# Taking a vector-matrix product off TensorE during a chunked scan: ACT scales the weight blocks, POOL adds them

## The reference, cut to what matters

```python
def second_block(x, c, w_mod, b_mod, g_mix_norm, ...):
    mod = jax.nn.silu(c) @ w_mod[l] + b_mod[l]        # (1, 1024) @ (1024, 6144)
    sh_m, sc_m, gt_m, sh_f, sc_f, gt_f = [m[:, None, :] for m in jnp.split(mod, N_MOD, axis=-1)]
    h = rms_norm(x, g_mix_norm[l]) * (1.0 + sc_m) + sh_m
```

## Time and profile before

| | us |
|---|---|
| runs | 1657.38, 1660.76, 1661.72 |
| profiled execution, its own time | 1656.79 |
| its span, first to last instruction | 1655.0 |
| PE busy over the span | 1355.6 |
| DVE busy | 1017.8 |
| ACT busy | 404.4 |
| POOL busy | 289.1 |
| scan of four chunks, from the first product to the last state | 204.1 to 354.5 |
| behind the scan, to the next block | 354.5 to 376.7 |

### The profile page before, as it was taken

One profiled execution on the slowest core, in us unless ns is written; L12 is line 12 of the kernel. 1 busy time (PEld: TensorE's weight loads), 2 busy tenths in 40 slices (PEclk: granted clock), 3 DMA queues, 4 the chain that ended last, 5 costly groups with the idle time before them and its releaser, 6 DMA issues. The chain is left out here.

```text
span 1655.0 us, 18102 instructions
## 1 busy us (share of the span) xinstructions
PE 1355.6 (82%) x6762; PEld 928.1 (56%) x6762; DVE 1017.8 (62%) x2352; ACT 404.4 (24%) x842; POOL 289.1 (17%) x297
## 2 busy tenths in 40 slices
PE   4796789997888787877877878765799968799988
PEld 2783477767853332332322223223688857699988
DVE  0597377774867868786868696542422487455542
ACT  1513300014521010101010101003523434554431
POOL 0002100000124343434443434420000000000000
PEclk9897798899899999999999999996899989899989
DMA  9346831137179999999999999992244205434543
GB/s 400 151 152 251 327 124 61 51 130 291 53 276 419 415 422 412 422 417 421 401 423 407 422 410 421 421 423 125 89 166 160 95 1 204 153 129 177 203 153 128
DMA packets 48184, 426.59 MB, mean 258 GB/s; under 512 B 5344, under 2 KB 5472, under 8 KB 5600
## 3 DMA queue, kind: packets, MB, share of 16 engines
q0 software_dynamic: 36864, 268.45, 39.4%
q1 hardware_dynamic: 11232, 156.98, 24.4%
HBM read 424.36 MB, written 1.05 MB: 257 GB/s over the span
## 5 line engine op out<-in xcount | busy, mean ns | idle before, releaser
L1232 PE MATMUL bank<-arena 128*128 128x512 f32 x1024 | 512.7, 638 | 151.6 <-DVE arena L1328 151.5
L1232 PEld LDWEIGHTS bank<-arena 128*128 128x128 f32 x1024 | 189.2, 199 | 470.2 <-DVE arena L1328 299.7
L1352 DVE CUSTOM_DVE_ANT_0 arena<-arena 128x1024 f32<-128x1024 f32 x256 | 313.1, 1223 | 176.0 <-DMA arena<-experts_in,arena 175.5
L1185 POOL DMA_INDIRECT arena<-experts_in,arena x256 | 268.3, 1048 | 629.1 <-PE bank L1232 373.5
L459 PE MATMUL bank<-rounded,rounded 128*128 128x256 f32 x1136 | 331.4, 292 | 56.3 <-DVE rounded L422 47.2
L460 PE MATMUL bank<-rounded,rounded 128*128 128x256 f32 x1136 | 328.0, 289 | 0.0
L461 PE MATMUL bank<-rounded,ring_r 128*128 128x256 f32 x1136 | 327.9, 289 | 0.0
L436 DVE TENSOR_TENSOR ring_r<-ring,rounded 128x1024 fp32r<-128x1024 f32 (+2 forms) x136 | 170.9, 1270 | 177.2 <-ACT rounded L431 177.2
L459 PEld LDWEIGHTS bank<-rounded,rounded 128*128 128x128 f32 x1136 | 223.6, 197 | 59.7 <-issue 38.2
L460 PEld LDWEIGHTS bank<-rounded,rounded 128*128 128x128 f32 x1136 | 224.4, 197 | 0.5 <-issue 0.5
L461 PEld LDWEIGHTS bank<-rounded,ring_r 128*128 128x128 f32 x1136 | 223.0, 196 | 0.0
(11 more groups left out here) (239 smaller groups left out, 1086.1 us busy)
## 6 DMA issues: line engine op xcount, KB each, us to landing
ring<-slots_in SPq DMA_DIRECT2D x73, 2048.0 KB, 8.4
arena<-experts_in,arena POOLq DMA_INDIRECT x256, 13.6
xT<-xT_in SPq DMA_DIRECT2D x1, 1024.0 KB, 15.8
mixT<-slots_in SPq DMA_DIRECT2D x1, 1024.0 KB, 6.8
out_dram<-xT SPq DMA_DIRECT2D x1, 1024.0 KB, 3.9
con<-consts_in SPq DMA_DIRECT2D x1, 552.0 KB, 13.7
vec<-vecs_in SPq DMA_DIRECT2D x1, 167.0 KB, 2.4
```

What stands on the lines that cost most here:

```text
L1185: pool.indirect_dma_start(rows[:, r % GRING, :], None, experts_in, bass.IndirectOffsetOnAxis(ap=expert[:, tt, at:at + 1], axis=0)).then_in ...
L1232: ins = pe.matmul(psum[2 * tt + half][:, :], diag[:, r % DIAGS, :], rows[:, r % GRING, D + 512 * half:D + 512 * half + 512], start=(h == 0 ...
L1352: dve.tensor_tensor_reduce(rows[:, r % GRING, 0:D], rows[:, r % GRING, 0:D], utok[:, tt, :], 1.0, 0.0, ALU.mult, ALU.add, hdot[:, r:r + 1] ...
```

## The change

The twelve product rows of the second modulation are no longer made by TensorE. ACT multiplies each 128x512 weight block by the vector's element of its partition: the product of block 0 goes into mrow, those of blocks 1 to 7 in turn into two buffers (gs_buf, in mixT[:, 4:8]). POOL adds each buffer to mrow, seven adds in a row of 84 in all, each behind a wait for the one before. When the seventh is done, POOL raises gv_out, and TensorE makes the same flips as before: for row 12 + 3c before step L3R of chunk c, for row 13 + 3c at its end, for row 11 + 3c behind step M2 (but not in chunk 0), and for row 23 at the very end. ACT frees a slot when its eight products are made. It does the Sqrt after all 96 products. DVE waits for all flips before it writes mixT[:, 4:8].

```diff
@@ PE's product rows, used now by the first modulation alone
-        def row_bank(q):
-            return 6 if 12 <= q < 18 else 5 + q % 2
...
-            if 13 <= q < 18:
-                pe.wait_ge(gv_out, q)
-            elif q >= 2:
+            if q >= 2:
                 pe.wait_ge(gv_out, q - 1)
@@ block of the scan
+        gs_prod, gs_sum = sem("gs_prod"), sem("gs_sum")
+        gs_buf = mixT[:, 4:8, :].rearrange("p (b c) t -> p b (c t)", b=2)
@@ POOL, behind its memsets
                 pool.memset(Ss, 0.0).then_inc(rc_zero, 1)
+                for j in range(12):
+                    for k in range(1, KT):
+                        a = 7 * j + k - 1
+                        pool.wait_ge(gs_prod, KT * j + k + 1)
+                        if a:
+                            pool.wait_ge(gs_sum, a)
+                        pool.tensor_tensor(mrow, mrow, gs_buf[:, a % 2, :], ALU.add).then_inc(gs_sum, 1)
+                    pool.wait_ge(gs_sum, 7 * (j + 1))
+                    pool.sem_inc(gv_out, 1)
@@ PE
-                pe_mod_row(pe, 12)
+                pe.wait_ge(rc_zero, 1)
                 pe.wait_ge(mod1_read, 1)
-                pe_mod_row(pe, 13)
-                pe_mod_cols(pe, 12)
-                pe_mod_row(pe, 14)
-                pe_mod_cols(pe, 13)
-                pe.wait_ge(rc_zero, 1)
                 for c in range(NC):
...
                     products(S.M2, [(part(RP[1], 1), part(WM[1], 1))])
+                    if c:
+                        pe_mod_cols(pe, 11 + 3 * c)
                     flip(S.TB, bd(BDb))
...
                         products(kw, [(part(RP[old], 1), both(WM[old]))], 2 * P)
+                    pe_mod_cols(pe, 12 + 3 * c)
                     products(S.L3R, [(part(WM[0], 1), part(RP[0], 0))])
...
-                    pe_mod_cols(pe, 14 + c)
-                    if c < NC - 1:
-                        pe_mod_row(pe, 15 + c)
+                    pe_mod_cols(pe, 13 + 3 * c)
 
                 pe.wait_ge(rc_ev, NC * S.COUNT)
-                pe_mod_row(pe, 18)
-                pe_mod_row(pe, 19)
-                pe_mod_cols(pe, 18)
-                pe_mod_row(pe, 20)
...
-                for q in (21, 22, 23):
-                    pe_mod_cols(pe, q - 2)
-                    pe_mod_row(pe, q)
-                pe_mod_cols(pe, 22)
                 pe_mod_cols(pe, 23)
@@ DVE
+                dve.wait_ge(gv_col, 24)
                 v(dve.tensor_tensor(mixT[:, 4:8, :], yT, gate, ALU.mult))
-                dve.wait_ge(gv_col, 24)
@@ ACT
-                for q in range(12, 19):
-                    act_mod_row(act, q)
+                for j in range(12):
+                    n = GV[12 + j][1]
+                    wait_slot(act, n)
+                    for k in range(KT):
+                        a = 7 * j + k - 1
+                        if k == 0:
+                            act.wait_ge(gv_col, 12 + j)
+                        elif a >= 2:
+                            act.wait_ge(gs_sum, a - 1)
+                        act.activation(mrow if k == 0 else gs_buf[:, a % 2, :], slot(n)[:, k, :], ACT.Copy,
+                                       scale=csil[:, 1, k, 0:1]).then_inc(gs_prod, 1)
+                    act.wait_ge(gs_prod, KT * (j + 1))
+                    act.sem_inc(slot_used[n % RING], 1)
                 act.wait_ge(rc_var, 1)
                 act.activation(st[:, 2], st[:, 1], ACT.Sqrt).then_inc(rc_sd, 1)
-                for q in range(19, 24):
-                    act_mod_row(act, q)
```

More of the change, by code:

```diff
@@ L240, in pe_mod_row @@
                 g = 32 * (k % 4)
-                ins = pe.matmul(psum[row_bank(q)][g:g + 32, :], csil[:, which, k, :], slot(n)[:, k, :],
+                ins = pe.matmul(psum[5 + q % 2][g:g + 32, :], csil[:, which, k, :], slot(n)[:, k, :],
                                 start=(k < 4), stop=(k >= 4))
@@ L257, in act_mod_row @@
                 act.wait_ge(gv_col, q)
-            act.copy(mrow, psum[row_bank(q)][:, :]).then_inc(gv_out, 1)
+            act.copy(mrow, psum[5 + q % 2][:, :]).then_inc(gv_out, 1)
         def pe_mod(pe, first, last):
```

## The result

The changed kernel takes 1687.11 us (median of 4 runs, 1685.46 to 1687.63) against 1659.07 for the kernel before (4 runs, 1657.11 to 1661.72): a ratio of 1.0166, 95% interval 1.0147 to 1.0185, so 28 us slower. The profiled execution took 1687.63, its span is 1685.8: 30.8 us above that of before. Forecast was 1680, range 1661 to 1694. The direction and the main cause came out; the size was 8 us short, and the terms were not all right.

What follows compares the result with a forecast made beforehand. The scan was taken as a PE-DVE ping-pong. Terms -1.2 - 5.6 + 3.4 + 4.5 + 0.6 + 17.2 + 1.0 = +19.9 us gave 1680.7 against the median 1660.76, stated as 1680; range 1661 to 1694.

Steps and rivals of the forecast that it cites:

- POOL beside DVE: In the scan, POOL's adds hold DVE's L963 (two SBUF inputs), later numbered L956, at chunk starts: +17.2 us.
- The step read from L633, L626 and L620: DVE instructions like L633 and L626 wait for POOL's instruction to end; L620, two SBUF inputs beside memsets, isn't held.
- Price of the add: POOL's add of 512 columns taken as 1.14 us plus 0.06 gap, 1.2 a step; bounds 0.52 and 1.39.
- The chain of a row: From one row's flips through ACT's products and POOL's seven adds to the next row ready: 10.8 us.
- Dates before L3R: Rows ready when PE reaches L3R: kept or late by 0.4 us, 0.2 taken in three chunks, +0.6 us.
- The first rival, POOL paces the scan: Add with wait of 1.45 us or more makes PE stand at flips before L3R: 1692 us and above, chance 0.18.
- The clock: PE's clock, which already drops at chunk starts, should cover the same dense work: given nothing.
- Start and boundaries: Scan starts earlier without three rows on PE, -1.2 us; DVE's wait at three chunk boundaries shrinks, -5.6 us.
- Flips inside the chunks: PE's flips before L3R in four chunks, 3.4 us, and after M2 in three, 4.5 us; bounds 0 to 9.4.
- Tail: After the scan: 4.2 us wait for flips goes, Sqrt and L1028 group start 5.2 late; net +1.0 us.
- adds of 1.39 and late flips: Slow-add case: 22 us for L963, 6 for late flips, 2.5 for the tail; +31.6, 1692.4 us.

Runs made afterwards that it cites:

- the first kernel with nine rows: Against the changed kernel: PE makes rows 12 to 14, ACT and POOL nine, flips placed by hand, L963's constant in PSUM; 1654.13 us, ratio 0.999 to the kernel before.

## Why the prediction was right or wrong

*POOL beside DVE: right.* The step read from L633, L626 and L620 held: L956 was held only while POOL read, 18.6 us against 17.2 forecast. It is the largest term, and taking it away gave 15 us back. Four held in the first chunk and six of eight in each other were forecast, and that is what the trace has. The size is close in part by luck. I had taken an add with its gap at 1.2 us and let each L963 that slipped through hold POOL for 0.25, which put the ends of adds 1.4 apart. The adds are longer, and L956 didn't hold POOL (9.74 us for seven adds with it, 9.78 without); the two errors together came out near the measured step of 1.42.

*Price of the add: mis-sized.* I took 1.14 us and 0.06 of gap; it is 1.27 and 0.15, a step of 1.42 and not 1.2. Two inputs of 512 cost more than the one of 1024 in its shorter row, 1.03. The estimate from the Trainium skill (GPSIMD Engine Reference, "3.1 Elementwise — side-by-side cycle accounting") was 1.12, further off. ACT's product is 0.72, not 0.61. The chain of a row came to 1.0 + 0.1 + 1.4 + 9.8 + 0.15 = 12.5, by the trace 258.65 to 271.12, where I had 10.8.

*Dates before L3R: the step that failed.* "M2 to L3R ... kept, or late by 0.4. I take 0.2 in three chunks: 0.6 us." It was late by 3.31, 1.60 and 0.33, 5.2 us. The first rival, POOL paces the scan, was thus half true; its condition, a step of 1.45 us, was missed by 0.03. Two things failed together. The chain took 12.5 us, and 13.1 where its flips ran at the lower clock (305.03 to 318.13), not 10.8. And PE came to L3R 9.2, 11.5 and 12.8 us after the start of the flips behind M2, where I had 10.4 and the flips: the date moves with the clock, and in the second chunk, where it is 1.00 from 260 to 268, PE is there first. The earlier trace rows shows 0.50 from 212 to 216, just ahead of that stretch.

*The clock: a term I set to nothing.* Behind these waits it cost 4.9 us. I had judged only the low stretch at a chunk's start, which is there before and after; that a new one can follow a wait of PE in the middle of a dense stretch I hadn't priced. Moving the flips, and the last chunk with the constant in PSUM, showed the two together.

*Start and boundaries: right.* -1.3 and -5.9 for -1.2 and -5.6.

*Flips inside the chunks:* 7.9 forecast, 7.1 left over in the account above. That remainder isn't measured by itself in the changed kernel; without the adds the same seven flips came to 9.2. (In the stretch of the earlier trace rows DVE idles 0.36 us more at 222.10, beside the 0.38 that I read; no term rests on it.)

*Tail: right in kind, short in size.* +1.0 forecast, +2.2 measured. The Sqrt came late as worked out: the L1021 group starts 12.0 us behind the first reduction, forecast 11.2, before 6.0. Two instructions of 128x16, one SBUF input each, L1012 and L1016, had been given nothing and took 0.94 and 1.27 in place of 0.17; they are of the kind of L626, and I had looked only for two inputs. L1014 took 2.17 in place of 1.22. Advancing the Sqrt gave nothing measurable.

Between the profiled executions the sum was 30.8 - 19.9 = 10.9 us short: the chain 4.6 (5.2 for 0.6), the clock 4.9, the held instructions 1.4, the tail 1.2, less 0.8 for the flips and 0.4 for start and boundaries. It stayed in the range because the upper end had been worked out with adds of 1.39 and late flips; that this also covered a clock term of 4.9 us that stood nowhere in the sum is luck.

## What to carry to other kernels

Before moving elementwise work to POOL, list the DVE instructions on the path that read two SBUF operands in that stretch, and the TENSOR_SCALAR ones from SBUF to SBUF. In this kernel those that met one of POOL's adds under way waited for its end, 0.29 us becoming up to 1.4; TENSOR_SCALAR was held by memsets too (L626), while TENSOR_REDUCE wasn't held beside the adds. Putting the constant operand of L956 in PSUM freed it, and was worth 15 us. Then compare the chain of a result with the shortest gap between the places where it is consumed, on the engine that waits, and count what the clock does behind a missed date. Remedies for the two don't add, because one makes the other's place wrong.

## What the runs showed of the hardware that I had not expected

- TensorE's clock fell to the lower level behind a wait of 1.6 us before L3R although PE was busy (0.50 from 323 to 327); behind a wait of 3.31 the loss was smaller (1.6 us against 3.3), and behind 0.33, 0.77 and 0.83 there was none. In the first kernel with nine rows it fell between 236 and 238 us with no wait of PE over 0.15 us in the 20 us ahead of it. What sets it off isn't settled by these runs.
- A DVE instruction of 128x16, 0.17 us, took 1.27 us beside POOL's adds: what it paid was the length of POOL's instruction, not its own.
- The other way round, only longer DVE instructions held POOL: six L956 among seven adds left them at 9.74 us, L1013 and L1014 of 1.23 us stretched seven adds to 11.52.
- Short memsets of POOL overlap: 35 of about 0.18 us each in 5.5 us.
